# A mixture-of-experts stage on one core: the table of passes in two parts, one piece of lookahead beside held buffers, and short blocks' products two pieces at a time

## What is computed

```
logits = h @ w_router                      # 384 tokens, 8 experts
top_v, top_i = top_k(logits, 2);  top_w = softmax(top_v)
y = sum over e of gates[e] * (silu(h @ wg[e]) * (h @ wu[e])) @ wd[e]
# h is 1024 wide, an expert's hidden width is 1792, all float32
```

## Time and profile before

| what | value |
|---|---|
| time, median of 3 runs | 1383.79 us (1382.92 to 1390.79) |
| time of the profiled execution | 1383.09 us |
| its span | 1381.2 us |
| PE busy | 1300.3 us, 94% of the span |
| DVE busy | 718.9 us, 52% |
| ACT busy | 525.1 us, 38% |
| stage of the experts | about 743 to 1340 us |

### The profile page before, as it was taken

One profiled execution on the slowest core, in us unless ns is written; L12 is line 12 of the kernel. 1 busy time (PEld: TensorE's weight loads), 2 busy tenths in 40 slices (PEclk: granted clock), 3 DMA queues, 4 the chain that ended last, 5 costly groups with the idle time before them and its releaser, 6 DMA issues.

```text
span 1381.2 us, 17263 instructions
## 1 busy us (share of the span) xinstructions
PE 1300.3 (94%) x6503; PEld 959.1 (69%) x6504; DVE 718.9 (52%) x1021; ACT 525.1 (38%) x632; POOL 120.5 (9%) x119
## 2 busy tenths in 40 slices
PE   5999999999999999999999799999789999999994
PEld 2555459999999854776558686654356778888882
DVE  1101565342432426554246874623335668898888
ACT  0101043332422232332125463522324557777772
POOL 0510005000000051000000000101002010202020
PEclk8999999999999999999996899999998999999997
DMA  9985474443342375511216774768966879999993
GB/s 366 359 323 214 174 283 138 153 164 109 108 165 91 117 277 179 211 33 70 98 67 232 242 247 162 255 244 317 367 233 213 310 281 378 368 371 392 372 352 150
DMA packets 125355, 317.09 MB, mean 230 GB/s; under 512 B 12931, under 2 KB 47078, under 8 KB 124774
## 3 DMA queue, kind: packets, MB, share of 16 engines
q1 hardware_dynamic: 119264, 295.00, 58.3%
q0 software_dynamic: 5744, 21.07, 5.0%
q10 hardware_dynamic: 278, 0.10, 0.0%
HBM read 306.37 MB, written 9.76 MB: 229 GB/s over the span
## 4 chain that ended last, share of the span: by engine, by line
PE 82%; DMA 7%; DVE 6%; SPq 2%; ACT 2%; issue 1%; DVEq 0%; ACTq 0%
PE ps L2526 9%; PE ps L2528 8%; PE ps L2527 8%; PE ps L2224 8%; PE ps L2226 8%; PE ps L2225 8%; PE ps L2189 7%; PE ps L2126 6%; PE ps L2532 5%; DMA sb_expert_raw<-in_moe_w_up 4%; PE ps L2316 3%; DVE sb_expert_w L1755 2%; DMA sb_ring<-in_ev_w_in 2%; PE ps L2086 2%; PE ps L2418 1%
## 5 line engine op out<-in xcount | busy, mean ns | idle before, releaser
L1755 DVE TENSOR_TENSOR sb_expert_w<-sb_expert_raw,sb_expert_w 128x1792 fp32r<-128x1792 f32 (+1 forms) x210 | 339.0, 1648 | 130.4 <-ACT sb_expert_w L1204 129.6
L1204 ACT CAST sb_expert_w<-sb_expert_raw 128x1792 fp32r<-128x1792 f32 (+1 forms) x210 | 287.1, 1392 | 178.9 <-DMA sb_expert_raw<-in_moe_w_down 88.4
L2526 PE MATMUL ps<-sb_expert_w,sb_expert_x 128*128 128x448 f32 x448 | 171.9, 384 | 27.5 <-DVE sb_expert_w L1755 16.7
L2527 PE MATMUL ps<-sb_expert_w,sb_expert_x 128*128 128x448 f32 x448 | 166.9, 373 | 0.0
L2528 PE MATMUL ps<-sb_expert_w,sb_expert_x 128*128 128x448 f32 x448 | 166.8, 372 | 0.0
L2526 PEld LDWEIGHTS ps<-sb_expert_w,sb_expert_x 128*128 128x128 f32 x448 | 86.5, 193 | 57.6 <-issue 34.2
L2224 PE MATMUL ps<-sb_split_acts,sb_split_weights 128*128 128x384 f32 x352 | 118.7, 337 | 0.4 <-issue 0.4
L2226 PE MATMUL ps<-sb_split_acts,sb_split_weights 128*128 128x384 f32 x352 | 118.4, 336 | 0.0
L2225 PE MATMUL ps<-sb_split_acts,sb_split_weights 128*128 128x384 f32 x352 | 118.4, 336 | 0.0
L2528 PEld LDWEIGHTS ps<-sb_expert_w,sb_expert_x 128*128 128x128 f32 x448 | 86.3, 193 | 7.7
L2527 PEld LDWEIGHTS ps<-sb_expert_w,sb_expert_x 128*128 128x128 f32 x448 | 86.6, 193 | 7.1
(11 more groups left out here) (334 smaller groups left out, 1830.5 us busy)
## 6 DMA issues: line engine op xcount, KB each, us to landing
sb_expert_raw<-in_moe_w_gate SPq DMA_DIRECT2D x128, 448.0 KB, 6.4
sb_expert_raw<-in_moe_w_up SPq DMA_DIRECT2D x128, 448.0 KB, 7.7
sb_expert_raw<-in_moe_w_down SPq DMA_DIRECT2D x112, 512.0 KB, 5.1
sb_ring<-in_ada_w SPq DMA_DIRECT2D x14, 3072.0 KB, 17.0
sb_ring<-in_ffn_w_gate SPq DMA_DIRECT2D x44, 256.0 KB, 3.7
sb_ring<-in_ffn_w_up SPq DMA_DIRECT2D x44, 256.0 KB, 4.7
sb_ring<-in_ffn_w_down SPq DMA_DIRECT2D x22, 512.0 KB, 6.2
sb_ring<-in_ev_w_in SPq DMA_DIRECT2D x4, 2048.0 KB, 14.9
```

The costliest lines, as they stand in the source:

```text
L1204: nc.scalar.copy(EWS[r][:, 0, 0:w], ERAW[:, r, 0:w]).then_inc(e_hi, 1)
L1755: V.tensor_tensor(EWS[r][:, 1, 0:w], ERAW[:, r, 0:w], EWS[r][:, 0, 0:w].bitcast(F32), ALU.subtract)\
L2526: first = mm(out, lh, rh, start=start, stop=False)
L2527: mm(out, lh, rl, start=False, stop=False)
```

## The change

There are three edits. (1) The table is made in two parts. A new `by_pass` finds the experts of the static passes and writes them early (tab_ready 1); the rest follows between `x_low(1)` and the split of pass 0's last piece (tab_ready 2). `expert_lows(0, 22, 22)` in the middle of it is empty. The loop count is read behind the static passes on all engines (on POOL and PE in the same way as on SP below). (2) PE does the products of two pieces with the full block and then those of the same two with the second block, where it alternated piece by piece; for down pieces this holds behind the first `spread(p)` ones. The signal that a piece is used then comes from its second block. (3) `pass_highs` and `pass_lows` use a lookahead of 1 instead of 4 where the pass or the one before it is in KEPT, which is passes 1 to 4.

```diff
@@ helpers @@
+        def ahead(p, before):
+
+            return 1 if p in KEPT or before in KEPT else 4
+
...
+        def order_ready(eng):
+
+            eng.wait_ge(tab_ready, 1)
+
         def more_items(eng):
 
-            eng.wait_ge(tab_ready, 1)
+            eng.wait_ge(tab_ready, 2)
             return eng.value_load(TAB[0:1, 0:1], min_val=1, max_val=TABLE - NS - 3)
...
@@ SyncE @@
-            more = more_items(sp)
+            order_ready(sp)
...
                 pass_loads(p, e_before, e)
                 e_before = e
+            more = more_items(sp)
             with sp.Fori(0, more) as j:
...
@@ ScalarE @@
             def pass_highs(p, before):
 
-                turn = KD + spread(before) + 4
-                expert_highs(p, 0, KD + 4)
+                more = ahead(p, before)
+                turn = KD + spread(before) + more
+                expert_highs(p, 0, KD + more)
                 gate_silu(p, 0)
-                expert_highs(p, KD + 4, turn)
+                expert_highs(p, KD + more, turn)
                 h_high(p, 0)
-                expert_highs(p, turn, KD + EB + 4)
+                expert_highs(p, turn, KD + EB + more)
                 y_out(before)
-                expert_highs(p, KD + EB + 4, 2 * KD + EB + 4)
+                expert_highs(p, KD + EB + more, 2 * KD + EB + more)
                 gate_silu(p, 1)
-                turn = min(ITEM_N, 2 * KD + EB + spread(p) + 4)
-                expert_highs(p, 2 * KD + EB + 4, turn)
+                turn = min(ITEM_N, 2 * KD + EB + spread(p) + more)
+                expert_highs(p, 2 * KD + EB + more, turn)
                 h_high(p, 1)
...
@@ VectorE @@
+            def by_pass():
+
+                ch(V.tensor_tensor(above, across(IX[:, 0:NE]), down_(cst("iota", 1)[:, 0:NE]), ALU.is_equal))
+                ch(V.tensor_tensor(above, above, across(cst("iota", 1)[:, 0:NE]), ALU.mult))
+                ch(V.tensor_reduce(FIRST, above, AX.X, ALU.add))
+                V.tensor_copy(TAB[:, 1:1 + NE], FIRST).then_inc(tab_ready, 1)
...
             by_rank(IX[:, 0:NE], "pass_of")
-            by_rank(CAP, "rows_of")
-            expert_lows(0, 4, 5)
-            left_over()
-            expert_lows(0, 5, 6)
+            by_pass()
+            order_ready(dve)
+            expert_lows(0, 4, 6)
             dve.wait_ge(h_stored, 16 * NG)
-            passes_of(0, cand("cand_expert"))
             expert_lows(0, 6, 7)
-            passes_of(1, FROM)
-            V.tensor_copy(TAB[:, :], TF).then_inc(tab_ready, 1)
-            more = more_items(dve)
             picked(0)
             select(1)
...
             x_low(1)
-            expert_lows(0, 2 * KD + 6, FIRST_N)
+            by_rank(CAP, "rows_of")
+            expert_lows(0, 2 * KD + 6, FIRST_N - 1)
+            left_over()
+            passes_of(0, cand("cand_expert"))
+            passes_of(1, FROM)
+            V.tensor_copy(TAB[:, 0:1], TF[:, 0:1])
+            V.tensor_copy(TAB[:, 1 + NE:], TF[:, 1 + NE:]).then_inc(tab_ready, 1)
+            expert_lows(0, FIRST_N - 1, FIRST_N)
             for p in range(1, NS):
                 pass_lows(p, p - 1)
+            more = more_items(dve)
...
@@ TensorE, gate_up @@
-                for k in range(KD):
+                def primary(k):
                     piece = e_piece(p, c0 + k)
                     piece_ready(piece)
                     first, last = gate_up_block(b, x, piece.r, k)
...
+                    elif not more_rows:
+                        last.then_inc(e_used, 1)
+
+                def secondary(k):
...
+                    _, last = gate_up_block(more_rows, XES2, e_piece(p, c0 + k).r, k)
+                    last.then_inc(gu_ps if k == KD - 1 else e_used, 1)
+
+                for k in range(0, KD, 2):
+                    primary(k)
+                    primary(k + 1)
                     if more_rows:
...
+                        secondary(k)
+                        secondary(k + 1)
...
@@ TensorE, down @@
-                for j in range(spread(p), EB):
-                    primary(j)
+                for j in range(spread(p), EB, 2):
+                    pair = range(j, min(j + 2, EB))
+                    for i in pair:
+                        primary(i)
                     if more_rows:
-                        secondary(j)
+                        for i in pair:
+                            secondary(i)
```

More of the change, by code:

```diff
@@ L961, in _ @@
             pool.wait_ge(h_stored, 16 * NG)
-            more = more_items(pool)
             n = 0
@@ L969, in _ @@
                     n += 1 + (p - 1 in SECOND)
+            more = more_items(pool)
             with pool.Fori(0, more) as j:
@@ L1807, in _ @@
             row = lambda a, n: MS[0:1, a:a + n]
+            FIRST = row(800, 8)
             KEY, RANK, IX, CAP, STARTS, FROM = row(300, 8), row(308, 8), row(316, CANDS), row(340, 8), row(348, 16), row(364, CANDS)
@@ L1923, in pass_lows @@
                 after = p + 1 if isinstance(p, int) else (p[0], p[1] + 1)
-                turn = KD + spread(before) + 4
+                more = ahead(p, before)
+                turn = KD + spread(before) + more
                 expert_lows(p, 0, 4)
                 select(after)
-                expert_lows(p, 4, KD + 4)
+                expert_lows(p, 4, KD + more)
                 hidden(p, 0)
-                expert_lows(p, KD + 4, turn)
+                expert_lows(p, KD + more, turn)
                 h_low(p, 0)
                 picked(after)
-                expert_lows(p, turn, 2 * KD + EB + 4)
+                expert_lows(p, turn, 2 * KD + EB + more)
                 hidden(p, 1)
-                turn = min(ITEM_N, 2 * KD + EB + spread(p) + 4)
-                expert_lows(p, 2 * KD + EB + 4, turn)
+                turn = min(ITEM_N, 2 * KD + EB + spread(p) + more)
+                expert_lows(p, 2 * KD + EB + more, turn)
                 h_low(p, 1)
@@ L2583, in gate_up @@
                         last.then_inc(gu_ps, 1)
-                    if more_rows:
-                        if k == 0 and u == 0:
-                            tokens_split(pe, p, 1)
-                        elif k == 0:
-                            hidden_split(pe, p, 0, 1)
-                        _, last = gate_up_block(more_rows, XES2, piece.r, k)
-                        if k == KD - 1:
-                            last.then_inc(gu_ps, 1)
-                    if k < KD - 1:
-                        last.then_inc(e_used, 1)
+                    elif not more_rows:
+                        last.then_inc(e_used, 1)
+                def secondary(k):
+                    if k == 0 and u == 0:
+                        tokens_split(pe, p, 1)
+                    elif k == 0:
+                        hidden_split(pe, p, 0, 1)
+                    _, last = gate_up_block(more_rows, XES2, e_piece(p, c0 + k).r, k)
[3 more added lines that the diff above has]
+                    primary(k + 1)
+                    if more_rows:
+                        secondary(k)
+                        secondary(k + 1)
             def down_block(b, h, col, r, start, stop):
@@ L2691, in _ @@
             gate_up(0, 0, 0, False)
-            more = more_items(pe)
+            order_ready(pe)
             pick(1)
@@ L2704, in _ @@
                 pass_products(p, p - 1)
+            more = more_items(pe)
             with pe.Fori(0, more) as j:
```

## The result

The changed kernel takes 1394.73 us (median of 13 runs, 1387.53 to 1402.02), the kernel before 1382.83 (13 runs). The ratio is 1.009, with a 95% interval of 1.0064 to 1.0116: +12.4 us, between +8.8 and +16.0, twice the +6.0 that was forecast. The profiled execution took 1396.15 us, its span is 1394.0.

What follows compares the result with a forecast made beforehand. The prediction took TensorE time to bound nearly everything from pass 1 on. Its terms 0.8 - 4.7 + 9.9 = +6.0 on 1383.1 us gave 1389.1, stated as 1389.8 for the median, range 1375 to 1395.

Steps and rivals of the forecast that it cites:

- Edit 1: Pass 0: table in two parts gains 6.9 us, then c22 waits 6.3 plus 1.4 at half clock; sum +0.8.
- Edit 2's 0.35 us a pair: Pass 1: each alternation of block products saved gives 0.35 us, 2.8 for 8 pairs; pass 3 taken at 0.24.
- Edit 3's nine larger waits: Passes 1, 3 and 4: PE waits before c9, c12, c16, c24, c27 of 1.3 to 2.3 us, 4.3 before c15.
- 0.6 for c9 of pass 2: Pass 2: c9, now split after the hidden columns, makes PE wait +0.6 us.
- The register loads behind pass 6: Loads moved behind pass 6: taken as 0, since DVE is ahead of PE there; upper bound 4.2 us.
- Rivals (2): Pass 0: table's second part is hidden at c22; -6.9 instead of +0.8, 1382.1 us; chance 0.15.
- (3): Lookahead costs nothing, PE not yet there when c9 and c24 come; its edit gives -4.5, 1375.5 us; chance 0.17.
- (4): Both the hidden table part and the costless lookahead hold; 1367.7 us; chance 0.08.
- edit 3's sum: Lookahead of one, passes 1 to 4: -4.5 + 4.65 + 1.45 + 0.6 + 1.3 + 2.0 + 4.35 = +9.9 us.
- rival (5): Slower by over 1%: half clock after six new waits of 2.0 to 2.4 us, up to +8.4, 1398; chance 0.10.
- the likeliest case: New waits of 1.4 to 2.4 us before c9, c12, c16, c24, c27 outweigh the saved ones; +6.0; chance 0.50.
- What c12 and c16 lose there: Pass 4, first half: losses of 0.8 and 1.8 us covered by DMA-bound c15 to c22; otherwise 2.6 more.

Runs made afterwards that it cites:

- e3: The kernel before with only the lookahead of 1 in passes 1 to 4; ratio to the kernel before 1.0119 (+16.4 us).
- again: The changed kernel profiled a second time with no edit; its stretches sum to +14.0 us against the first profile of the kernel before.
- e9: The kernel before with only the lookahead of 1 in passes 1 to 4, y_out staying behind the cast of c18; ratio 1.0065 (+9.0 us).
- e6: The changed kernel with y_out back behind the cast of c18; ratio to the kernel before 1.0034 (+4.7 us).
- e10: Changed kernel, table's second part between pass 1's c3 to c6 splits, lookahead 1 only in pass 3's first half, down pieces alternating; ratio 0.9898, 1370.51 us.

## Why the prediction failed

**Right.** The direction, and that it is the lookahead which costs. Edit 1: +0.5 for +0.8, with the turn, the wait at c22 and the half clock behind it each within 0.5 us. Edit 2's 0.35 us a pair in pass 1; in pass 3 it is 0.3 where 0.24 was taken (two pieces in 4.40 + 2.54 us, 2 x 3.63 before). Edit 3's nine larger waits within 0.5 us; the smallest term, 0.6 for c9 of pass 2, came to nothing. The register loads behind pass 6 cost nothing that shows: passes 6 and 7 changed by less than 0.1 us. Rivals (2), (3) and (4) fell: PE did wait at c22, c9 and c24.

**Wrong, by 5.5 us in the profile.** The mechanism was right, its price was half of what was measured (+6.0 for +12.4 in the runs, +11.5 in the profile). The step that failed is edit 3's sum, +9.9 where e3 measured +16.4: it charged the new waits with their own length and nothing for half clock behind them, and it took c16's wait in pass 4 as covered. The stretches of the table where the time lies point at four places:

1. Half clock was charged once, behind c22 (1.4), and for the waits of 2 us handed to rival (5), on the ground that one gap of 2.10 us was followed by full clock. One row was no ground. Behind c16's wait it cost 1.3 us in both profiles of after; in the second half of pass 4, where only c24 and c27 wait, the stretch cost 4.6, 7.7, 6.2, 7.7 and 6.1 us (after, again, e3, e9, e6) against 4.35, as half clock came not at all, twice, once, twice and once. The mean is 6.5, so 2.1 belonged into the sum there, though the first profile of after shows only 0.3 of it. Rival (5)'s mechanism was at work, at part of its price, inside the likeliest case.
2. "What c12 and c16 lose there (0.8, 1.8) is covered by the DMA-bound c15 to c22 behind them": c16's isn't. The likely reason, argued from the order and not measured, is that the casts and splits that y_out holds up also free the slots for the loads. Pass 4's c0 to c23 cost 3.5 instead of 2.0, and with y_out late the same stretch, c9's wait included, costs nothing. The cover was there for c9 and not for c16; the prediction had it the other way round.
3. The pairs' late release was counted at nothing with the argument that the chain of transfers starts before these pairs. The alternation of e10 gave 1.5 us back before c8 of pass 2. Against it stood the down pairs' own gain, 0.7 in pass 1 and 0.7 in pass 2, which was left out too. Both omissions nearly cancel, so that the term was near nothing is luck and not its argument.
4. All stretches bound by transfers were taken from one profile of before, which was 3.5 us shorter in the experts' stage than the next. Passes 2 and 3 stand 2.7 us above the forecast in the first profile of after. This may be no more than the drift; the runs don't show it.

The measured median of 1394.73 us lies just inside the range, 1375 to 1395, and that too is luck: the range had its upper end at "the forecast with edit 2 at nothing". Steps 1 and 2 are both of edit 3, where no upper bound was taken, although a rival was made of one of them.

## What to carry to other kernels

A lookahead in front of a join isn't spare: cut from four pieces to one it became waits of 1.1 to 2.3 us in front of eight pieces here. And each wait of about 2 us on the TensorE should carry an expected price for half clock beside its own length, here about 1 us (six times in ten, 1.6 us each). When an order is shifted by one constant, look at every instruction that it moves, above all those that themselves wait for the engine at the end of the chain (y_out here): with slack before it such an instruction's place didn't show in the time here, without slack it holds up all that is queued behind. And work that is off the path is hidden only where the engine that does it is ahead: the table's 7.5 us cost 6 us before the last piece of pass 0 and nothing five pieces later.

## What the runs showed of the hardware

Whether a wait of 1.86 to 2.33 us is followed by half clock is not a property of its length: the same wait of the same kernel, 1.86 us before c9, left the granted clock at 1.00 in one profile and at 0.53 in the next. Behind idle times of 4.3 to 9.4 us (c15 of pass 3, in every profile) the first six products took 2.22 to 2.38 us instead of 1.3. In the second half of pass 4 a stretch of half clock cost 1.6 us wherever it fell, often not in the first products behind the wait but in the piece after. The two profiles of the kernel before, equal to 0.4 us as long as PE or DVE set the pace, differed by up to 1.6 us in a stretch that waits for transfers, with the same order of loads: two profiles of before would have shown that ahead of the forecast.
